# Attention seam of a two-block model: queries evacuated between rotations, two value banks taken by ACT, the mask between the kinds of score matmul

## The chip, the cores and the metric

The kernel runs on one core of one Trainium2 chip. The time is device microseconds of one execution, the median of three runs. Engines are named as in the profile: PE is TensorE (PEld its weight loads), DVE is VectorE, ACT is ScalarE, POOL is GpSimd, SP is SyncE, which issues most of the DMAs.

## The reference

A sequence of 512 tokens of width 1024 goes through two blocks in fp32. The first has an HGRN2 mixer with a gated convolution and a convolutional FFN. The second has two layers, each of FFN, mixer, FFN; the mixer of its first layer is a causal pooling, that of its second is multi-head latent attention. The change touches only this attention:

```python
cq = rmsnorm_2(u @ w_dq, q_lora_norm)                    # 512 x 256
q = jnp.einsum('bsr,rhd->bshd', cq, w_uq)                # 16 heads, 128 plain + 64 rope
q_nope = q[..., :QK_NOPE_DIM]
q_rope = apply_rope(q[..., QK_NOPE_DIM:], cos[None, :, None], sin[None, :, None])
...
s = (jnp.einsum('bqhd,bkhd->bhqk', qn_b, k_nope)
     + jnp.einsum('bqhr,bkr->bhqk', qr_b, k_rope))
s = s.astype(jnp.float32) * scale
s = jnp.where(mask[None, None], s, -jnp.inf)             # causal
p = jax.nn.softmax(s, axis=-1).astype(v.dtype)
return jnp.einsum('bhqk,bkhd->bqhd', p, v)
```

Keys and values come from a shared latent of 128 columns (`k_nope`, `v`), and one rope key of 64 is shared by all heads.

## The kernel before, in words

Every engine runs one hand-written program of its own, in order, and meets the others at counting semaphores. An instruction that waits holds all that stands behind it on its engine.

The 16 heads are done in four quarters of four heads, `attend(q)` on each engine, the first three in a loop (q is a register there) and the last written out (q is the integer 3, and `last` is true). A quarter has 14 groups of matmuls, each filling one of eight PSUM banks and counted by `groups_done`: two groups of rope queries and four of keys, computed at the end of the quarter before, then in `attend` four of values (numbers 6 to 9, in banks 6, 7, 0, 1) and four of queries (10 to 13, in banks 2 to 5). A product of fp32 data with split operands (`three`) is three matmuls, a high and a low part of each side, so a value group is three matmuls and a query group six. DVE empties the banks and counts them in `evacuated`; PE waits for that count before it reuses a bank.

The rope queries of two pairs of heads take a path of their own. DVE evacuates them to `QRr` (`take_rope`) and multiplies by the cosines into `QRt` (`rope_cosines`). SP turns the 32-row blocks of `QRr` into `QRs` with four DMAs (`turn_queries`, L618). DVE multiplies `QRs` by the sines (L2842) and adds it to `QRt` (L2846), which is the rotation. ACT writes the high part of the rotated queries (`rope_queries_hi`, L1286 and L1287), DVE the low part (`rope_queries_lo`, L2815), and SP joins the halves of each pair with two DMAs (`join_halves`, L624 and L626), counted by `rope_moved`. `rope_q` holds cosines and sines; the sign of two blocks of sines is turned once by DVE (L2796).

Score tile i of a head is 128 queries by (i+1)*128 keys in ring bank i: a plain product in fp32 (L2027, recorded as two matmuls), two rope matmuls (high and low key, L2030), and a bf16 matmul that adds the causal mask to the last block (L2032). DVE takes the maximum of each row (L2859) and scales it (L2862), ACT takes the exponential with its sum (L1315), DVE the reciprocal (L2868) and normalises (L2873), PE transposes the probabilities (L2061), DVE and ACT copy them to SBUF, and PE multiplies by the values (L2078). PE writes scores of head h+1 into a ring bank once the exponential of head h has read it.

Between its rope copies and its first exponential, ACT also converts the weights of the next quarter in the first three quarters:

```python
rope_queries_hi(q)
if not isinstance(q, int):
    rope_hi(q * 2 + (UB["attn"] + 3), q + 1, q * 14 + (GB["attn"] + 6))
    a.wait_ge(groups_done, q * 14 + (GB["attn"] + 14))
    keys_hi(q * 2 + (UB["attn"] + 2), q + 1, 0, UNIT, 4)
```

`keys_hi` (L1266, waited for at L1306) overwrites the high parts from which this quarter's values and queries are computed. POOL subtracts them from the raw weights to get the low parts (`rope_lo` L665, `split_lo` L672).

Of the kernel before, what the change touches and what calls it, by code (L numbers as in the profile page):

```python
# [9 lines left out]
ACT = mybir.ActivationFunctionType  # L10
# [119 lines left out]
def build(nc, A, out):  # L130
    ctx = ExitStack()
    with ctx:
# [238 lines left out]
        rope_key_ready = sem("rope_key_ready")  # L371
        scores_ready = sem("scores_ready")
# [107 lines left out]
        def _(sp):  # L480
# [132 lines left out]
            def turn_queries(q, taken):  # L613

                sp.wait_ge(evacuated, taken)
                for b in range(4):
                    src, dst = slice(b * 32, b * 32 + 32), slice((b ^ 1) * 32, (b ^ 1) * 32 + 32)
                    sp.dma_start(QRs[dst, :], QRr[src, :]).then_inc(qrope_turned, 16)  # L618
# [14 lines left out]
            turn_queries(0, GB["attn"] + 6)  # L633
# [147 lines left out]
        def _(a):  # L781
# [518 lines left out]

            def attend(q):

                rope_queries_hi(q)
# [68 lines left out]
        def _(pe):  # L1372
# [612 lines left out]
            def attend(q):  # L1985
# [25 lines left out]
                for x in range(4):  # L2011
                    queries(x, 10 + x)

                def scores(h, i0=0, i1=TC):

                    if h % 2 == 0:
                        pe.wait_ge(rope_moved[h // 2], q * 32 + 32)
                    for i in range(i0, i1):
                        if i == i0:
                            pe.wait_ge(evacuated, q * 14 + (gb + 11 + h))  # L2020
                        if h == 0:
                            if i == 3:
                                pe.wait_ge(evacuated, q * 14 + (gb + 12))
                        else:
                            pe.wait_ge(exp_ready, q * 16 + (4 * (h - 1) + i + 1))
                        n = (i + 1) * P
                        nc.tensor.matmul(ring[i][:, 0:n], QN[:, h * T + i * P:h * T + (i + 1) * P],  # L2027
                                         KN[:, h * T:h * T + n], start=True, stop=False)
                        for key in rope_key:
                            nc.tensor.matmul(ring[i][:, 0:n], rope_two[h][:, i * P:(i + 1) * P], key[:, 0:n],  # L2030
                                             start=False, stop=False)
                        nc.tensor.matmul(ring[i][:, i * P:n], identb[:, :], causal[:, :],  # L2032
                                         start=False, stop=True).then_inc(scores_ready, 1)
# [16 lines left out]
                scores(0)  # L2050
                for h in range(4):
                    if h < 3:
                        scores(h + 1, 0, TC - 1 if h < 2 else TC)
                    if h == 0:
                        pe.wait_ge(evacuated, q * 14 + (gb + 14))
                    for i in range(TC):
# [42 lines left out]
        def _(v):  # L2099
# [694 lines left out]
            for b in (0, 2):  # L2794
                minus = rope_q[b * 32:b * 32 + 32, T:2 * T]
                nc.vector.tensor_scalar(minus, minus, -1.0, None, ALU.mult).then_inc(sin_signed, 1)  # L2796

# [27 lines left out]
            rope_cosines(0, 4)  # L2825

            def attend(q):
# [7 lines left out]
                def take_values(n):  # L2835
                    v.wait_ge(groups_done, q * 14 + (gb + n + 1))
                    nc.vector.tensor_copy(tile(VV, n - 6), banks[n % 8][:, :]).then_inc(evacuated, 1)

                v.wait_ge(qrope_turned, q * 64 + 64)
                v.wait_ge(sin_signed, 2)  # L2840
                for j in range(2):
                    nc.vector.tensor_tensor(tile(QRs, j), tile(QRs, j), rope_q[:, T:2 * T], ALU.mult  # L2842
                                            ).then_inc(qrope_part, 1)
                for j in range(2):
# [3 lines left out]
                for j in range(2):  # L2848
                    take_values(6 + 2 * j)
                    take_values(7 + 2 * j)  # L2850
                    rope_queries_lo(q, j)
                for j in range(4):
                    take(10 + j, tile(QN, j))
# [22 lines left out]
                maxes(0)  # L2876
                normalise(0)
# [130 lines left out]
```

## Time and profile before

| | |
|---|---|
| median of three runs | 2347.74 us (2346.78 to 2347.82) |
| profiled execution | 2345.91 us, its span 2344.0 us |
| mean granted TensorE clock | 0.996 |
| PE busy | 2308.6 us (98%) |
| PEld busy | 2016.7 us (86%) |
| DVE busy | 1665.8 us (71%) |
| ACT busy | 1020.1 us (44%) |
| POOL busy | 841.4 us (36%) |

Busy time is a share of the whole span, and the attention is only its part from about 1716 to 1899 us. The quarters start their value groups at about 1718.7, 1770.2, 1814.4 and 1858.7 us. In a timeline a row is one instruction, or several of one kind in a row (xN): its start, its duration, and in brackets the idle time before it with what ended it. The duration of an instruction covers its passage through the engine, and the next one of the same engine can start a little before it is over.

### The profile page before, as it was taken

The page shows a single profiled execution, that of the slowest core. Times are in us where ns is not written, and L with a number is a line of the kernel's source. Part 1 is how long each engine was busy: PE and PEld are TensorE (multiplying, and loading weights), DVE is VectorE, ACT ScalarE, POOL GpSimd, SP SyncE. Part 2 cuts the span into 40 slices and gives each one's busy share as a digit, 9 for nine tenths or more (in the row PEclk, how much of TensorE's full clock was granted, in tenths as well). Part 3 has the DMA queues.
Part 4 walks back from the last instruction along what each step waited for, and adds up shares of the span by engine and source line. Part 5 has one row for each costly group of instructions (what it writes and reads, how often), then busy time and mean ns, then how long its engine had stood idle before and what let it go on. Part 6 is the DMA issues. An engine that isn't in the chain of part 4 may idle for free.

```text
span 2344.0 us, 33535 instructions
## 1 busy us (share of the span) xinstructions
PE 2308.6 (98%) x13510; PEld 2016.7 (86%) x13510; DVE 1665.8 (71%) x1672; ACT 1020.1 (44%) x1294; POOL 841.4 (36%) x441
## 2 busy tenths in 40 slices
PE   9999999999999999999999999999989999999998
PEld 7888788888789999979899879899967778899997
DVE  6687687772489678668587769696777743686874
ACT  5324443432355344554354454353444443453443
POOL 1321222121046446349256228356310001474561
PEclk9999999999999999999999999999999999999999
DMA  5221232332323333323342333332332222233322
GB/s 176 72 72 55 73 111 93 100 96 95 97 73 118 99 111 95 102 73 103 113 126 73 91 117 98 102 122 93 91 77 50 62 73 90 90 101 112 113 86 86
DMA packets 221332, 221.39 MB, mean 94 GB/s; under 512 B 11154, under 2 KB 217617, under 8 KB 221201
## 3 DMA queue, kind: packets, MB, share of 16 engines
q1 hardware_dynamic: 221040, 219.46, 29.8%
q8 instruction: 96, 1.57, 0.3%
q14 instruction: 36, 0.29, 0.0%
q10 hardware_dynamic: 160, 0.07, 0.0%
HBM read 213.22 MB, written 2.10 MB: 92 GB/s over the span
## 4 chain that ended last, share of the span: by engine, by line
PE 84%; POOL 5%; DVE 5%; issue 2%; ACT 2%; DMA 2%; SPq 0%; DVEq 0%; ACTq 0%; POOLq 0%
PE bank L1385 15%; PE bank L1387 15%; PE bank L1386 15%; PE bank L1379 10%; PE bank L1381 10%; PE bank L1380 10%; POOL sums L697 2%; POOL raw L698 1%; PE bank L2078 1%; PE bank L1514 1%; POOL sums L700 1%; PE bank L2027 1%; POOL sums L702 1%; PE bank L2030 1%; PE bank L2061 1%
## 5 line engine op out<-in xcount | busy, mean ns | idle before, releaser
L1379 PE MATMUL bank<-Xhi,wlo 128*128 128x256 f32 (+1 forms) x1283 | 374.2, 292 | 4.3 <-DVE Xlo L2382 2.8
L1380 PE MATMUL bank<-Xlo,whi 128*128 128x256 f32 (+1 forms) x1283 | 373.0, 291 | 0.0
L1381 PE MATMUL bank<-Xhi,whi 128*128 128x256 f32 (+1 forms) x1283 | 372.9, 291 | 0.0
L697 POOL TENSOR_TENSOR sums<-raw 128x512 f32<-128x512 f32 x72 | 147.2, 2044 | 430.5 <-DMA raw<-in_ffn_post_wg_dram 162.5
L1060 ACT ACTIVATE whi<-raw 128x2048 fp32r<-128x2048 f32 x72 | 138.3, 1921 | 370.5 <-PE bank L1387 230.7
L1379 PE MATMUL bank<-Xhi,sxlo 128*128 128x256 f32 (+1 forms) x960 | 281.0, 293 | 0.4 <-ACT kept L1099 0.2
L1380 PE MATMUL bank<-Xlo,sxhi 128*128 128x256 f32 (+1 forms) x960 | 278.9, 291 | 0.0
L1381 PE MATMUL bank<-Xhi,sxhi 128*128 128x256 f32 (+1 forms) x960 | 278.8, 290 | 0.0
L1379 PEld LDWEIGHTS bank<-Xhi,wlo 128*128 128x128 f32 x1283 | 241.8, 188 | 11.7 <-issue 4.5
L1380 PEld LDWEIGHTS bank<-Xlo,whi 128*128 128x128 f32 x1283 | 241.7, 188 | 6.5 <-issue 0.5
L1381 PEld LDWEIGHTS bank<-Xhi,whi 128*128 128x128 f32 x1283 | 241.8, 188 | 5.8
L1385 PE MATMUL bank<-xghi,wlo 128*128 128x512 f32 x592 | 232.3, 392 | 0.8 <-DVE work L2426 0.4
L2473 DVE TENSOR_TENSOR wlo<-raw,whi 128x2048 fp32r<-128x2048 f32 x72 | 211.4, 2937 | 30.2 <-ACT whi L1060 29.6
L1387 PE MATMUL bank<-xghi,whi 128*128 128x512 f32 x592 | 230.5, 389 | 0.0
L792 ACT ACTIVATE whi<-raw 128x2048 fp32r<-128x2048 f32 x68 | 130.1, 1913 | 224.2 <-PE bank L1387 224.0
L1386 PE MATMUL bank<-xglo,whi 128*128 128x512 f32 x576 | 224.2, 389 | 0.0
L2104 DVE TENSOR_TENSOR wlo<-raw,whi 128x2048 fp32r<-128x2048 f32 x55 | 127.2, 2312 | 128.9 <-ACT whi L792 128.9
L2566 DVE SCALAR_TENSOR_TENSOR xT<-bank,xT 128x512 f32<-128x512 f32 x128 | 86.2, 687 | 168.8 <-PE bank L1387 168.8
L1379 PEld LDWEIGHTS bank<-Xhi,sxlo 128*128 128x128 f32 x960 | 180.4, 188 | 6.2 <-ACT kept L1099 1.3
L1380 PEld LDWEIGHTS bank<-Xlo,sxhi 128*128 128x128 f32 x960 | 180.4, 188 | 4.8 <-issue 0.5
L1381 PEld LDWEIGHTS bank<-Xhi,sxhi 128*128 128x128 f32 x960 | 180.4, 188 | 4.4
L2476 DVE TENSOR_TENSOR sxlo<-sums,sxhi 128x1536 fp32r<-128x1536 f32 x72 | 174.2, 2420 | 0.0
(389 smaller groups left out, 5597.4 us busy)
## 6 DMA issues: line engine op xcount, KB each, us to landing
raw<-in_ffn_w_up_dram SPq DMA_DIRECT2D x22, 1024.0 KB, 5.1
raw<-in_ffn_pre_wg_dram SPq DMA_DIRECT2D x22, 1024.0 KB, 5.3
raw<-in_ffn_pre_wu_dram SPq DMA_DIRECT2D x22, 1024.0 KB, 5.4
raw<-in_ffn_post_wg_dram SPq DMA_DIRECT2D x22, 1024.0 KB, 5.4
raw<-in_ffn_post_wu_dram SPq DMA_DIRECT2D x22, 1024.0 KB, 5.4
raw<-in_ffn_pre_wd_dram SPq DMA_DIRECT2D x24, 768.0 KB, 4.8
raw<-in_ffn_post_wd_dram SPq DMA_DIRECT2D x24, 768.0 KB, 4.8
raw<-in_w_in_dram SPq DMA_DIRECT2D x13, 1024.0 KB, 5.0
```

What stands on the lines that cost most here:

```text
L697: nc.gpsimd.tensor_tensor(s1, a21, a22, ALU.add).then_inc(adds_done[h], 1)
L792: nc.scalar.activation(whi[:, s * UNIT:(s + 1) * UNIT], raw[:, s * UNIT:(s + 1) * UNIT], ACT.Copy).then_inc(whi_ready[s], 4)
L1060: nc.scalar.activation(whi[:, h * UNIT:(h + 1) * UNIT], raw[:, h * UNIT:(h + 1) * UNIT], ACT.Copy).then_inc(whi_ready[h], 2)
L1379: nc.tensor.matmul(bank, wl, x, start=first, stop=False, skip_group_check=True)
L1380: nc.tensor.matmul(bank, w, xl, start=False, stop=False, skip_group_check=True)
L1381: return nc.tensor.matmul(bank, w, x, start=False, stop=last, skip_group_check=True)
L1385: nc.tensor.matmul(bank, wlo_, xhi, start=first, stop=False)
L1386: nc.tensor.matmul(bank, whi_, xlo, start=False, stop=False)
L1387: return nc.tensor.matmul(bank, whi_, xhi, start=False, stop=last)
L2104: nc.vector.tensor_tensor(wlo[:, c], raw[:, c], whi[:, c].bitcast(F32), ALU.subtract).then_inc(wlo_ready[s], 4)
L2473: nc.vector.tensor_tensor(wlo[:, c], raw[:, c], whi[:, c].bitcast(F32), ALU.subtract).then_inc(wlo_ready[h], 2)
L2476: nc.vector.tensor_tensor(sxlo[h][:, :], sums[h][:, :], sxhi[h][:, :].bitcast(F32), ALU.subtract).then_inc(wlo_ready[h], 2)
```

## The change

On PE, three of the four query groups stand before the scores of head 0 and the fourth (`queries(3, 13)`) behind them. Each score tile is plain product, mask, rope matmuls, and the wait for the joined rope halves has moved from ahead of the head to ahead of the first tile's rope matmuls. On DVE the values 8 and 9 are taken first (each counts 2 in `evacuated`), then rotation 0, query 0, rotation 1, low part 0, query 1, low part 1, query 2; query 3 is taken behind the maxima of head 0. Each rotation is a multiply followed at once by its add. ACT takes the values 6 and 7 at the head of `attend`, counted by the new semaphore `values_act`, for which PE waits before it transposes head 0. In quarter 0 ACT issues two of the four turning DMAs. The turning of the signs moves behind `rope_cosines`. Nothing else is edited.

```diff
-            turn_queries(0, GB["attn"] + 6)
+            turn_queries(0, GB["attn"] + 6, (0, 1))
...
+            a.wait_ge(evacuated, GB["attn"] + 6)
+            for b in (2, 3):
+                src, dst = slice(b * 32, b * 32 + 32), slice((b ^ 1) * 32, (b ^ 1) * 32 + 32)
+                nc.scalar.dma_start(QRs[dst, :], QRr[src, :]).then_inc(qrope_turned, 16)
+
             def attend(q):
 
+                for n in (6, 7):
+                    a.wait_ge(groups_done, q * 14 + (GB["attn"] + n + 1))
+                    nc.scalar.activation(tile(VV, n - 6), banks[n][:, :], ACT.Copy).then_inc(values_act, 1)
                 rope_queries_hi(q)
...
-                for x in range(4):
+                for x in range(3):
                     queries(x, 10 + x)
...
-                    if h % 2 == 0:
-                        pe.wait_ge(rope_moved[h // 2], q * 32 + 32)
...
-                        for key in rope_key:
-                            nc.tensor.matmul(ring[i][:, 0:n], rope_two[h][:, i * P:(i + 1) * P], key[:, 0:n],
-                                             start=False, stop=False)
                         nc.tensor.matmul(ring[i][:, i * P:n], identb[:, :], causal[:, :],
+                                         start=False, stop=False)
+                        if h % 2 == 0 and i == i0:
+                            pe.wait_ge(rope_moved[h // 2], q * 32 + 32)
+                        nc.tensor.matmul(ring[i][:, 0:n], rope_two[h][:, i * P:(i + 1) * P], rope_key[0][:, 0:n],
+                                         start=False, stop=False)
+                        nc.tensor.matmul(ring[i][:, 0:n], rope_two[h][:, i * P:(i + 1) * P], rope_key[1][:, 0:n],
                                          start=False, stop=True).then_inc(scores_ready, 1)
...
                 scores(0)
+                queries(3, 13)
...
                         pe.wait_ge(evacuated, q * 14 + (gb + 14))
+                        pe.wait_ge(values_act, q * 2 + 2)
...
-            for b in (0, 2):
-                minus = rope_q[b * 32:b * 32 + 32, T:2 * T]
-                nc.vector.tensor_scalar(minus, minus, -1.0, None, ALU.mult).then_inc(sin_signed, 1)
...
             rope_cosines(0, 4)
+            for b in (0, 2):
+                minus = rope_q[b * 32:b * 32 + 32, T:2 * T]
+                nc.vector.tensor_scalar(minus, minus, -1.0, None, ALU.mult).then_inc(sin_signed, 1)
...
-                v.wait_ge(qrope_turned, q * 64 + 64)
-                v.wait_ge(sin_signed, 2)
-                for j in range(2):
+                def rotate(j):
                     nc.vector.tensor_tensor(tile(QRs, j), tile(QRs, j), rope_q[:, T:2 * T], ALU.mult
                                             ).then_inc(qrope_part, 1)
-                for j in range(2):
                     v.wait_ge(qrope_part, q * 4 + (j + 3))
                     nc.vector.tensor_tensor(tile(QRt, j), tile(QRt, j), tile(QRs, j), ALU.add
                                             ).then_inc(qrope_ready, 1)
-                for j in range(2):
-                    take_values(6 + 2 * j)
-                    take_values(7 + 2 * j)
-                    rope_queries_lo(q, j)
-                for j in range(4):
-                    take(10 + j, tile(QN, j))
+
+                take_values(8)
+                take_values(9)
+                v.wait_ge(qrope_turned, q * 64 + 64)
+                v.wait_ge(sin_signed, 2)
+                rotate(0)
+                take(10, tile(QN, 0))
+                rotate(1)
+                rope_queries_lo(q, 0)
+                take(11, tile(QN, 1))
+                rope_queries_lo(q, 1)
+                take(12, tile(QN, 2))
...
                 maxes(0)
+                take(13, tile(QN, 3))
                 normalise(0)
```

## Rows read from the trace of the kernel before

**Rows 1.** PE's waits over the whole span: total us, times, longest.
```profile
PE bank L2027 <- DVE QN L2833: 9.0, 4, 6.7
```
**Rows 2.** Timeline of PE, quarter 0: start us, us, instruction, idle before.
```profile
1733.73 0.80 PE L2027 MATMUL bank<-KN,QN 128*128 128x128 f32 x2 [6.72 <-DVE QN L2833]
```
**Rows 3.** Windows: stretch, length, busy PE, PEld, DVE, ACT, POOL, clock, DMA, GB/s.
```profile
1733.70:1736.00 2.30, 2.27 (x9) 2.09 (x9) 2.12 (x5) 0.11 (x1) 2.30 (x1) 0.50 0.49 114
...
635.00:636.00 1.00, 1.00 (x6) 1.00 (x6) 1.00 (x2) 0.64 (x2) 0.00 (x0) 0.50 0.00 0
```
**Rows 4.** Timeline of PE ahead of the second of those windows.
```profile
633.47 0.36 PE L1379 MATMUL bank<-Xhi,wlo 128*128 128x256 f32 x1 [2.80 <-DVE Xlo L2382]
```
**Rows 5.** Timeline of PE, quarter 1.
```profile
1772.95 0.39 PE L1385 MATMUL bank<-cqhi,wlo 128*128 128x512 f32 x1
...
1778.16 0.39 PE L1387 MATMUL bank<-cqhi,whi 128*128 128x512 f32 x1
1779.49 0.49 PE L2027 MATMUL bank<-KN,QN 128*128 128x128 f32 x2 [0.94 <-DVE QN L2833]
...
1783.41 0.44 PE L2027 MATMUL bank<-KN,QN 128*128 128x128 f32 x2
...
1789.25 2.39 PE L2078 MATMUL bank<-PT,VV 128*128 128x512 f32 x8 [0.31 <-DVE PT L2883]
```
**Rows 6.** Timeline of DVE, quarter 1.
```profile
1771.67 1.28 DVE L2842 TENSOR_TENSOR work<-work,rope_q 128x512 f32<-128x512 f32 x2
...
1775.27 0.69 DVE L2815 TENSOR_TENSOR work<-QRt,whi 128x512 fp32r<-128x512 f32 x1
...
1777.06 1.77 DVE L2815 TENSOR_TENSOR work<-QRt,wlo 128x512 fp32r<-128x512 f32 x1
...
1785.34 0.18 DVE L2868 RECIPROCAL rowinv<-rowsum 128x4 f32<-128x4 f32 x1 [0.85 <-ACT work L1315]
```
**Rows 7.** Timeline of ACT, quarter 1.
```profile
1773.59 0.63 ACT L1286 ACTIVATE whi<-QRt 128x512 fp32r<-128x512 f32 x1 [3.87 <-DVE QRt L2846]
...
1778.73 1.91 ACT L1266 ACTIVATE whi<-raw 128x2048 fp32r<-128x2048 f32 x1 [1.88 <-PE bank L1387]
1781.65 0.37 ACT L1315 ACTIVATE work<-bank,negmax 128x128 f32<-128x128 f32 x1 [1.01 <-DVE negmax L2862]
...
1784.53 0.69 ACT L1315 ACTIVATE work<-bank,negmax 128x512 f32<-128x512 f32 x1 [0.91 <-DVE negmax L2862]
```
**Rows 8.** Timeline of SP, quarter 1 (DMA issues).
```profile
1776.52 0.60 SPq L626 DMA_DIRECT2D whi<-work  x1
```
**Rows 9.** DMA issues, quarter 1: count, KB each, median us to landing.
```profile
whi<-work SPq DMA_DIRECT2D x2, 128.0 KB, 2.2
```
**Rows 10.** Timeline of POOL, quarter 1.
```profile
1780.78 4.55 POOL L672 TENSOR_TENSOR wlo<-raw,whi 128x2048 fp32r<-128x2048 f32 x1 [2.50 <-ACT whi L1266]
```
**Rows 11.** Timeline of POOL and DVE in the first block.
```profile
136.82 2.28 POOL L741 TENSOR_TENSOR V<-fkb 128x1024 f32<-128x1024 f32 x1 [10.57 <-DVE SC L2192]
...
137.38 2.00 DVE L2208 TENSOR_SCALAR CH<-GC,cols 128x512 f32<-128x512 f32 x1
```
**Rows 12.** One line of the kernel: durations in ns, min/median/max.
```profile
L2862 DVE TENSOR_SCALAR negmax<-rowmax x64: 153/154/156, 1735.7 to 1891.5; 128x1 f32<-128x1 f32 x64
```
**Rows 13.** Timeline of DVE and SP, quarter 0.
```profile
1715.69 0.85 DVE L2796 TENSOR_SCALAR rope_q<-rope_q 32x512 f32<-32x512 f32 x2
...
1721.01 3.21 SPq L618 DMA_DIRECT2D work<-sq  x4
...
1725.94 1.29 DVE L2842 TENSOR_TENSOR work<-work,rope_q 128x512 f32<-128x512 f32 x2 [3.76 <-DMA work<-sq]
...
1741.12 0.18 DVE L2868 RECIPROCAL rowinv<-rowsum 128x4 f32<-128x4 f32 x1 [0.85 <-ACT work L1315]
```
**Rows 14.** Timeline of DVE and PE, quarter 3.
```profile
1860.12 1.29 DVE L2842 TENSOR_TENSOR work<-work,rope_q 128x512 f32<-128x512 f32 x2
...
1877.03 2.39 PE L2078 MATMUL bank<-PT,VV 128*128 128x512 f32 x8 [0.19 <-DVE PT L2883]
```

More of the change, by code:

```diff
@@ L371, in build @@
         rope_key_ready = sem("rope_key_ready")
+        values_act = sem("values_act")
         scores_ready = sem("scores_ready")
@@ L611, in quarter_weights, with turn_queries @@
                              heads(1, NOPE, NOPE + ROPE)).then_inc(raw_ready[1], 16)
-            def turn_queries(q, taken):
+            def turn_queries(q, taken, blocks=range(4)):
                 sp.wait_ge(evacuated, taken)
-                for b in range(4):
+                for b in blocks:
                     src, dst = slice(b * 32, b * 32 + 32), slice((b ^ 1) * 32, (b ^ 1) * 32 + 32)
@@ L2836, in take_values @@
                     v.wait_ge(groups_done, q * 14 + (gb + n + 1))
-                    nc.vector.tensor_copy(tile(VV, n - 6), banks[n % 8][:, :]).then_inc(evacuated, 1)
-                v.wait_ge(qrope_turned, q * 64 + 64)
-                v.wait_ge(sin_signed, 2)
-                for j in range(2):
+                    nc.vector.tensor_copy(tile(VV, n - 6), banks[n % 8][:, :]).then_inc(evacuated, 2)
+                def rotate(j):
                     nc.vector.tensor_tensor(tile(QRs, j), tile(QRs, j), rope_q[:, T:2 * T], ALU.mult
                                             ).then_inc(qrope_part, 1)
-                for j in range(2):
                     v.wait_ge(qrope_part, q * 4 + (j + 3))
```

## The prediction, made before the change was run

> **What bounds the kernel now.** The page's busy times come first: PE is busy nearly throughout, every other engine much less (the table above). Time can come only from PE's idle time or from fewer PE cycles, and the change removes no matmul. The list of PE's waits over the whole span says where the idle time is: the largest is the first score matmul (L2027) waiting for DVE's queries, 9.0 us in four waits, 6.7 of it in one [rows 1]. That is the seam of each quarter of the attention, where the last query matmul ends and the first score waits.
>
> PE's timeline shows the seam of quarter 0: 6.72 us idle before the first score at 1733.73 [rows 2]. The granted clock behind it is 0.50, the lower of the two levels (1.2 GHz), and an idle time of 2.80 us at another place is also followed by 0.50 [rows 3, 4]. In quarter 1 the seam costs 0.94 us [rows 5]. I take quarter 1 as the model. DVE is busy without a break from 1771.67 to the first score, so DVE's order sets when scores start. After that one chain matters: scores, maxima, exponentials on ACT, reciprocal (1785.34) and normalising on DVE, transposes, and the first probability-value product (L2078) at 1789.25 [rows 5, 6]. I measure each quarter by how far its reciprocal, or that product, moves; behind the product PE has no wait worth a line until the next seam.
>
> **PE's new order.** Three query groups stand before the scores of head 0 and the fourth after them. From 1772.95 to 1778.16 are 23 spacings of 0.227 us, so one group of six matmuls is 1.36 us [rows 5]: PE is through three at 1777.03, and the moved group puts 1.36 us between the scores of heads 0 and 1. Head 0's four tiles take 3.92 us (1779.49 to 1783.41) [rows 5].
>
> **The mask between the kinds.** Same matmuls, same weights, other order. No row has the new order; I take 0. Bounds: a quarter of one 0.227 us spacing, either way, on the 16 one-block tiles, where the matmuls are too short to cover a weight load: 1 us.
>
> **DVE's new order, quarter 1.** DVE is free at 1771.67 [rows 6]. It now first wants values 8 and 9, whose last matmuls start 0.91 and 0.23 us before 1772.95 and last 0.39. The copies start at about 1772.5 and 1773.2: free at 1773.8. Two operations in a row take 0.60 and 0.69 (1.28), and one that waits for its predecessor's result must let the whole 0.69 pass [rows 6], so a rotation, now a multiply and at once its add, is 1.33 us. Rotation 0 ends at 1775.15, query 0 at 1775.75, rotation 1 at 1777.08, and the low part of rotated pair 0 at 1777.77; before it ended at 1775.27 + 0.69 = 1775.96 [rows 6]. It is 1.8 us later although ACT now takes two value banks, because it has moved behind two copies that must first be waited for, a query and the other rotation. ACT has its high part ready at about 1776.6 (from 1775.28, two copies of 0.65) and doesn't hold it; ACT's two value copies end by 1772.4 and lie in the 3.87 us that it idled [rows 7]. The low part of pair 1 would start at 1778.55 before POOL's short subtraction and lose the stretch that made it 1.77 us [rows 6]; head 2 alone wants it, so nothing comes of that.
>
> **The halves arrive late.** After the low part SP issues two transfers, the second 0.56 us behind it, and a landing takes 2.2 us, 2.3 with the wake-up behind it [rows 6, 8, 9]: 1777.77 + 0.56 + 2.3 = 1780.65. PE, ready at 1777.03, does tile 0's plain product and mask (some 0.4 us) and stands until 1780.7: 3.1 us idle. The remaining 3.6 of the 3.92 us follow: head 0's scores end at S = 1784.3, before at 1783.41.
>
> **The wait that nobody moved.** In quarters 0 to 2 ACT converts the next quarter's weights (L1266, 1.91 us) ahead of its first exponential, and waits for group 14 of the quarter, the last query (L1306). It waited for PE before as well, 1.88 us, and started 0.18 us after the last query's end (1778.16 + 0.39) [rows 5, 7], with time to spare. Now that query is computed behind the scores. Behind the waiting ACT stand all exponentials of head 0, and for each of them PE's next tile of head 1, which reuses the bank. S 1784.3, + 1.52 (last query's end), + 0.18, + 1.83 for the conversion: ACT is free at 1787.85. The exponentials, 0.37 us for the smallest tile and 0.69 for the largest, with 0.09 each for reading the sum, are 2.5 us for four in a row [rows 7]; the reciprocal starts at 1790.35 instead of 1785.34: **+5.0 us**. Query 3's evacuation on DVE (0.69) hides in DVE's own wait for these.
>
> **POOL comes into step with normalising.** POOL's subtraction starts 0.14 us after the conversion and lasts 4.55 us [rows 7, 10]. Before it ended at 1785.33, as normalising began. Now it runs from 1788.0 to 1792.6, and normalising would start at 1790.6. Bounds: the scaling of the maxima, a TENSOR_SCALAR of one column, took 0.153 to 0.156 us in all 64 cases, beside POOL too [rows 12]: 0. A TENSOR_SCALAR of 512 columns from SBUF to SBUF, started at 137.38 beside a POOL operation that ended at 139.10, took 2.00 us and ended 0.28 after it [rows 11]: then normalising waits until 1792.6, **+2.0**. That row is nearer (many columns, SBUF to SBUF), so I take 2.0. The Trainium skill (SBUF — State Buffer, Who interferes with whom) has a rule for it: GpSimd and a VectorE operation in a two-port mode shut each other out for a whole instruction, and tensor_scalar is among those that can enter the mode. By that rule the 2.0 us stand, without it the sum would be 6.0 us less; the trace agrees in the 2.00 us row.
>
> **The clock.** Idle times of 6.72 and 2.80 us were followed by work at 0.50, the 0.94 us of quarter 1 was not [rows 2 to 5]. From first score to reciprocal quarter 0 took 7.39 us (1733.73 to 1741.12), quarter 1 5.85 (1779.49 to 1785.34) [rows 2, 5, 6, 13]: 1.5 us for one fall. The 3.1 us idle time makes one in quarters 1, 2 and 3, +1.5 each; bounds 0 and, as PE stands for another 2.5 us behind the moved query, 3.0.
>
> **Quarters.** *1 and 2:* 5.0 + 2.0 + 1.5 = 8.5 each. *3* has no conversion behind it. From DVE's start at 1860.12 the same steps land the halves at 1869.1 and end the scores at 1872.8. Then PE is the path: 1.36 for the query, and what quarter 1 took from there to the product (1783.41 to 1789.25, 5.84) less 0.6 of waiting in it: 1879.4, before 1877.03 [rows 5, 14]. +2.3, and +1.5 for the clock: 3.8. *0:* the two sign operations (0.85) leave the front of DVE's chain, so the rope queries are evacuated 0.9 us earlier, at 1720.1. Two of the four turning transfers go to ACT's queue, where ACT is idle; four issues took 3.21 us, two fewer save 1.3, and the turned halves are there at about 1724.0 instead of 1725.94 [rows 13]. The Trainium skill (DMA: Bandwidth & Descriptors, Issuing engines are not separate DMA queues) says that all issuers share the same DMA engines and a second one saves issue time only. By that the 1.3 us is all there is to have; no run here has two issuers. The same steps give: low part done 1727.95, halves landed 1730.8, scores (with the lower clock, as before) until 1736.0, ACT free 1739.5, reciprocal 1742.0 against 1741.12: +0.9, and +2.0 for POOL. The conversion eats what this quarter gained.
>
> **Sum.** 2.9 + 8.5 + 8.5 + 3.8 = 23.7 us. The profiled run took 2345.91 us for its span of 2344.0; the median of the runs is 2347.74, 1.8 above it. 2347.7 + 23.7 = 2371.4, taken as 2371.
>
> **Rivals.**
> *POOL and normalising do not meet:* +23.7 - 6.0 = +17.7, 2365.4. For it the one-column row, against it the 2.00 us row. 0.18.
> *The conversion is not on the path,* if ACT gets through it in time. Quarters 1 to 3 then go as the last, 3.8 each, and quarter 0, bound by PE from 1736.0 on, has its product at 1742.6, 2.4 earlier than the 1745.0 that its reciprocal implies: +9.0, 2356.7. Against it: the waiting instruction stands ahead of the exponentials. 0.07; in half of it, without the clock falls, +4.5, within 0.2%.
> *PE is never held* (the other side): quarter 0 gives back 6.7 and 1.5, and each other quarter its seam and some 0.6 behind it, 5 in all: 2334. Its place is the wait for the rope halves ahead of tile 0's last two matmuls. It decides from the point where they land when three queries are done, 1777.0 in quarter 1 and not 1780.65. Against it: their low part isn't computed until 1777.8. 0.04.
> The forecast has the rest, 0.71, with a range of its own of 2366 to 2378.
>
> **How the numbers follow.** A measurement of this kernel can tell about 0.2%, 4.7 us, from no change. Low end: no meeting with POOL (-6.0), no clock falls (-4.5), mask -1: +12.2, 2360, and 2358 to take in some of the small rivals. High end: a second fall in each quarter (+6), landings 0.6 us slower in each (+2.4), mask +1: +33, cut to 2380, since they won't all come. Slower 0.92, same 0.04 (half the second rival), faster 0.04.
>
> **What the profile after would show.** L1266 starting behind the head-0 scores in quarters 0 to 2, the first exponential right behind it; PE idle for about 3 us at tile 0's rope matmul and about 2.5 us at head 1's first tile, released by ACT; the first normalising instruction of those quarters stretched to 1 to 2 us; a clock below 1 in every quarter; quarter 0 about even. The prediction is wrong if the first exponential does not wait behind L1266, or if quarter 1's low part of pair 0 ends by 1776 and no rope wait shows.

## The result and the profile after

The changed kernel takes 2370.2 us (median of 4 runs, 2366.59 to 2378.85) against 2347.78 (4 runs, 2346.78 to 2347.98): a ratio of 1.0099, 95% interval 1.0076 to 1.0122. It is slower by 22.4 us; the forecast was 2371. The profiled execution took 2366.59 us for a span of 2364.8, 20.8 more than before's.

All of it is in the attention's four quarters. The table gives the start (us) of each quarter's first probability-value product (L2078 before, L2090 after); for quarter 3 it gives the start of the output projection behind it instead. What a quarter adds is the growth of the lag between the two kernels since the quarter ahead of it. Quarter 0's figure adds the 0.31 us by which this trace starts the values of quarter 0 earlier (1718.38 against 1718.69).

| quarter | before | after | this quarter adds | forecast |
|---|---|---|---|---|
| 0 | 1745.03 | 1750.05 | 5.3 | 2.9 |
| 1 | 1789.25 | 1801.10 | 6.8 | 8.5 |
| 2 | 1833.48 | 1852.29 | 7.0 | 8.5 |
| 3 | 1898.45 | 1919.52 | 2.3 | 3.8 |

PE's waits over the whole span of the changed kernel (total us, times, longest), in the place of the one wait of before [rows 1]:
```profile
PE bank L2040 <- DMA whi<-work: 14.0, 4, 4.3
PE bank L2034 <- ACT work L1324: 7.5, 3, 2.5
PE bank L2073 <- DVE work L2887: 2.2, 3, 1.8
...
PE bank L2034 <- DVE QN L2844: 0.8, 1, 0.8
```
The wait for DVE's queries is nearly gone (9.0 to 0.8 us). What stands in its place is larger: 14.0 us for the rotated halves, once in each quarter, and 7.5 us for ACT, once in each of quarters 0 to 2.

PE's timeline of quarter 1 after the change, to be laid beside [rows 5]; this quarter starts 5.00 us later than before's:
```profile
1782.03 0.38 PE L2034 MATMUL bank<-KN,QN 128*128 128x128 f32 x2
1782.25 0.22 PE L2036 MATMUL bank<-causal,identb 128*128 128x128 bf16 x1
1785.67 0.33 PE L2040 MATMUL bank<-whi 128*128 128x128 f32 x1 [3.20 <-DMA whi<-work]
...
1789.32 0.39 PE L1394 MATMUL bank<-cqhi,wlo 128*128 128x512 f32 x1
...
1793.34 0.49 PE L2034 MATMUL bank<-KN,QN 128*128 128x128 f32 x2 [2.49 <-ACT work L1324]
...
1797.83 1.55 PE L2073 MATMUL bank<-ident,work 128*128 128x128 f32 x10 [0.20 <-DVE work L2887]
```
PE does tile 0's plain product and its mask and then stands 3.20 us until the halves land. The moved query starts at 1789.32, which is where head 0's scores end. Head 1's first tile then waits 2.49 us for an exponential.

ACT, POOL and DVE in the same stretch, to be laid beside [rows 6, 7, 10]:
```profile
1791.03 1.91 ACT L1267 ACTIVATE whi<-raw 128x2048 fp32r<-128x2048 f32 x1 [6.90 <-PE bank L1396]
1792.85 0.35 ACT L1324 ACTIVATE work<-bank,negmax 128x128 f32<-128x128 f32 x1
...
1793.08 4.52 POOL L673 TENSOR_TENSOR wlo<-raw,whi 128x2048 fp32r<-128x2048 f32 x1 [7.55 <-ACT whi L1267]
...
1782.08 0.68 DVE L2823 TENSOR_TENSOR work<-QRt,whi 128x512 fp32r<-128x512 f32 x1
...
1795.01 0.18 DVE L2882 RECIPROCAL rowinv<-rowsum 128x4 f32<-128x4 f32 x1 [3.43 <-ACT work L1324]
1795.22 3.46 DVE L2887 TENSOR_SCALAR work<-work,rowinv 128x128 f32<-128x128 f32 x4
```
ACT stood 6.90 us in front of the conversion, where before it stood 1.88, and the first exponential runs right behind it. DVE then waits 3.43 us for the exponentials instead of 0.85. Normalising takes 3.46 us instead of 1.27. The line's own durations in that quarter (ns, min/median/max) say how:
```profile
L2887 DVE TENSOR_SCALAR work<-work,rowinv x4: 341/441/2467, 1795.2 to 1798.2; 128x128 f32<-128x128 f32 x1, 128x256 f32<-128x256 f32 x1, 128x384 f32<-128x384 f32 x1, 128x512 f32<-128x512 f32 x1
```
One of the four took 2.47 us, from 1795.22 to 1797.69, and POOL's subtraction ended at 1793.08 + 4.52 = 1797.60; the others were not held.

Windows of the changed kernel, columns as in [rows 3]. The first two are in quarter 1, head 0's scores and the later part of head 1's (behind the 2.49 us wait); the third is a stretch of quarter 0 behind the same wait, the last the whole attention:
```profile
1785.70:1789.30 3.60, 3.60 (x17) 2.46 (x18) 1.73 (x6) 0.00 (x0) 0.00 (x0) 1.00 0.21 50
1795.30:1797.80 2.50, 2.33 (x6) 1.03 (x5) 2.50 (x2) 0.00 (x0) 2.31 (x1) 0.54 0.00 0
...
1747.00:1750.00 3.00, 3.00 (x8) 1.69 (x8) 1.67 (x5) 2.33 (x8) 0.00 (x0) 0.53 0.90 255
...
1715.00:1925.00 210.00, 183.59 (x862) 132.89 (x861) 145.02 (x327) 89.50 (x212) 17.35 (x6) 0.96 0.20 54
```
Behind 3.20 us of idle time the scores of quarter 1 ran at full clock. The fall came after the second wait, and there it cost nothing: PE, though slowed, still stood 0.20 us at the transposes (L2073) for normalising, which POOL was holding up. At full clock it would only have stood there longer, 1.79 us (experiment 6). In quarter 0 the clock fell twice, and the second fall reached the transposes and the product.

### The profile page after: what moved, and what is told of

Its sections match the earlier page's. It is cut to its first block, busy times and chain, and to the rows that moved or that the text cites. A ratio compares the mean times of both kernels' runs of the same rounds, so it can differ in the third digit from the quotient of the medians.

```text
span 2364.8 us, 33547 instructions
## 1 busy us (share of the span) xinstructions
PE 2314.5 (98%) x13510; PEld 2020.5 (85%) x13510; DVE 1669.4 (71%) x1664; ACT 1022.1 (43%) x1302; POOL 842.0 (36%) x441
## 4 chain that ended last, share of the span: by engine, by line
PE 84%; POOL 5%; DVE 4%; DMA 2%; issue 2%; ACT 2%; SPq 0%; DVEq 0%; ACTq 0%; POOLq 0%
PE bank L1394 16%; PE bank L1396 16%; PE bank L1395 16%; PE bank L1388 10%; PE bank L1389 10%; PE bank L1390 10%; POOL sums L698 2%; POOL raw L699 1%; PE bank L2090 1%; PE bank L2034 1%; PE bank L1523 1%; POOL sums L701 1%; POOL sums L703 1%; PE bank L2073 1%; PE bank L2040 0%
```

## The experiments

Each was timed against the kernel before in the same session (medians of before 2347.32, 2347.6 and 2347.48). The question behind them: which edits cost, which gain, and does a version exist that keeps the gain?

**1. One edit alone.** The kernel before, with only the fourth query group moved.
```diff
-                for x in range(4):
+                for x in range(3):
                     queries(x, 10 + x)
...
                 scores(0)
+                queries(3, 13)
...
-                for j in range(4):
+                for j in range(3):
                     take(10 + j, tile(QN, j))
...
                 maxes(0)
+                take(13, tile(QN, 3))
```


> The kernel before, with one edit: query 3 is computed behind the scores of head 0 and evacuated behind their maxima. Main theory (the weight conversion L1266, which waits for that query, holds the exponentials): quarter 1 keeps its first score at the old distance, its reciprocal comes about 4.1 us later (1.52 to the last query's end, 0.18, 1.83 for the conversion, 2.5 for four exponentials, against 1.9 before), and the normalising meets POOL for 2.2 us more: +6.3 us in each of quarters 0 to 2, about +0.7 in the last: +19 to +20, 2367 (up to 3 more by the clock). Rival (the late halves are what costs, and filling PE with a query behind the scores is harmless): -1 to +2, 2346 to 2350.

Measured: 2368.32 us (2366.61 to 2372.21), ratio 1.0089 (1.0074 to 1.0105). This edit by itself costs 21.0 us, where the whole change costs 22.4. Its DVE timeline, quarter 1, shows both waits:
```profile
1795.13 0.18 DVE L2869 RECIPROCAL rowinv<-rowsum 128x4 f32<-128x4 f32 x1 [3.43 <-ACT work L1315]
1795.34 3.45 DVE L2874 TENSOR_SCALAR work<-work,rowinv 128x128 f32<-128x128 f32 x4
```
The rivals in which the conversion is not on the path fall.

**2. The same edit undone.** The changed kernel, with the query back ahead of the scores.
```diff
-                for x in range(3):
+                for x in range(4):
                     queries(x, 10 + x)
...
                 scores(0)
-                queries(3, 13)
```


> The changed kernel with query 3 computed ahead of the scores again; its evacuation stays behind the maxima. Main theory: PE does the query inside its 3.2 us wait for the halves, ACT converts before the first score, POOL is done before the normalising. What is left is the lateness of the halves: +0.9 in quarters 1 and 2, +1.5 in 3, -2 in 0: about +1, 2349 (2346 to 2351). Rival (late halves and the ACT value copies are the cost): the 3.2 us idle time per quarter stays on the path: 2360 or more.

Measured: 2351.16 us (2349.25 to 2353.73), ratio 1.0017 (1.0008 to 1.0026): 19 us come back. The reciprocal of quarter 1 waits for little:
```profile
1786.75 0.18 DVE L2881 RECIPROCAL rowinv<-rowsum 128x4 f32<-128x4 f32 x1 [0.21 <-ACT work L1324]
```
That is 2 us above what was expected. All the other edits together (with query 3 still evacuated behind the maxima) are a small loss of 3.8 us. PE's waits name it:
```profile
PE bank L2040 <- DMA whi<-work: 10.0, 4, 4.3
```

**3. The order on ACT alone.** The changed kernel, the conversion and its wait moved behind head 0's exponentials; PE's order stays as changed.
```diff
-                    a.wait_ge(groups_done, q * 14 + (GB["attn"] + 14))
-                    keys_hi(q * 2 + (UB["attn"] + 2), q + 1, 0, UNIT, 4)
...
                 exps(0)
+                if not isinstance(q, int):
+                    a.wait_ge(groups_done, q * 14 + (GB["attn"] + 14))
+                    keys_hi(q * 2 + (UB["attn"] + 2), q + 1, 0, UNIT, 4)
```


> The changed kernel with ACT's conversion of the next quarter's weights moved behind the exponentials of head 0; query 3 stays behind the scores. Main theory (the place of the conversion in ACT's queue is the cost, and not the late query): reciprocal of head 0 back to about 1.9 us behind the scores, PE bound by its own work from there, POOL now beside the normalising of head 1 for up to 1 us: +2.3 in quarter 3, +2 to +3 in 1 and 2, about 0 in 0: 2354 to 2357 against 2370. Rival (the late query is the cost wherever the conversion is): no gain, 2366 or more.

Measured: 2354.37 us (2352.21 to 2355.0), ratio 1.0028 (1.0016 to 1.0039). So 16 us come back without touching PE's order: it is not the late query that costs, but the exponentials queued behind an instruction that waits for it. Head 1's first tile no longer waits for ACT. POOL, which follows the conversion, no longer meets normalising either, which is back at 1.27; the 16 us hold both:
```profile
1787.84 1.27 DVE L2888 TENSOR_SCALAR work<-work,rowinv 128x128 f32<-128x128 f32 x4
```

**4. POOL out of step.** The changed kernel, POOL's subtraction held back until head 0 is normalised.
```diff
                 rope_lo(q * 2 + (UB["attn"] + 3))
+                pool.wait_ge(probs_ready, q * 16 + 4)
                 split_lo(q * 2 + (UB["attn"] + 2), 0)
```


> The changed kernel; POOL's subtraction waits until head 0 is normalised. Main theory (the two can't run together): the first normalising instruction of quarters 0 to 2 goes back from about 2.5 us to 0.29, -2.2 in each, -6.6: 2363 to 2365. Rival (the stretched instruction hides behind the other work or has another cause): no change, 2370.

Measured: 2367.12 us (2363.96 to 2368.41), ratio 1.0082 (1.0068 to 1.0096), 3.1 us below the changed kernel's first median and 3.9 below its second (experiment 7). The mechanism is there: in quarter 1 POOL starts at 1794.06, behind normalising, and that takes its 1.28.
```profile
1792.65 1.28 DVE L2888 TENSOR_SCALAR work<-work,rowinv 128x128 f32<-128x128 f32 x4
```
But of the 3 x 2.19 = 6.6 us only about half comes back in the medians, and the two traced spans differ by 2.7 us. The traces say where the rest went. From head 1's first tile to the first product the quarters 0 to 2 took 8.93, 7.76 and 7.76 us in the changed kernel and take 5.58, 6.71 and 5.58 here. Where no fall touches either kernel (quarter 2) that is the 2.19 us less; quarter 0 gains more, since the changed kernel had a fall there, and quarter 1 less, since PE at the lower clock now has no wait to hide in. Together it is 6.6 us less. But in quarter 2 the clock now falls behind the wait for the halves, where it did not in the changed kernel's trace. These are PE's rope matmul and the 6 us from there on, first in this kernel, then in the changed one (window columns as above):
```profile
1833.21 0.47 PE L2041 MATMUL bank<-whi 128*128 128x128 f32 x1 [3.26 <-DMA whi<-work]
1833.20:1839.20 6.00, 5.99 (x15) 3.62 (x16) 1.74 (x6) 0.00 (x0) 0.00 (x0) 0.50 0.12 29
...
1836.85 0.33 PE L2040 MATMUL bank<-whi 128*128 128x128 f32 x1 [3.26 <-DMA whi<-work]
1836.80:1842.80 6.00, 5.18 (x23) 3.43 (x23) 3.28 (x9) 0.58 (x1) 0.00 (x0) 1.00 0.14 31
```
After the same 3.26 us of idle time one ran at 0.50 and the other at 1.00. From this rope matmul to head 1's first tile it took 10.75 us here and 7.68 there, so the fall gave back 3.1 us. Whether falls also explain the medians is not shown: the two kernels' falls differ from run to run.

**5. The mask alone.** The kernel before, with the mask between the kinds and the wait at the first tile's rope matmuls.
```diff
-                    if h % 2 == 0:
-                        pe.wait_ge(rope_moved[h // 2], q * 32 + 32)
                     for i in range(i0, i1):
...
-                        for key in rope_key:
-                            nc.tensor.matmul(ring[i][:, 0:n], rope_two[h][:, i * P:(i + 1) * P], key[:, 0:n],
-                                             start=False, stop=False)
                         nc.tensor.matmul(ring[i][:, i * P:n], identb[:, :], causal[:, :],
-                                         start=False, stop=True).then_inc(scores_ready, 1)
+                                         start=False, stop=False)
+                        if h % 2 == 0 and i == i0:
+                            pe.wait_ge(rope_moved[h // 2], q * 32 + 32)
+                        nc.tensor.matmul(ring[i][:, 0:n], rope_two[h][:, i * P:(i + 1) * P], rope_key[0][:, 0:n],
+                                         start=False, stop=False)
+                        nc.tensor.matmul(ring[i][:, 0:n], rope_two[h][:, i * P:(i + 1) * P], rope_key[1][:, 0:n],
+                                         start=False, stop=True).then_inc(scores_ready, 1)
```


> The kernel before with two edits: the mask between the plain product and the rope matmuls, and the rope wait ahead of the first tile's rope matmuls. In the changed kernel's trace the new order takes 0.04 us more on a one-block tile, 0.03 more on two blocks, nothing on three and 0.02 less on four; the wait is not what ends last before the scores of quarters 0 to 2. Main theory: no difference, within 1 us. Rival (the switch between kinds costs or saves weight loads): 3 us either way over the 64 tiles.

Measured: 2347.95 us, ratio 1.0 (0.9991 to 1.0009). The mask's new place costs and gives nothing that an interval of 2 us either way would show. (11 of its 12 executions lie between 2346.41 and 2350.5 us; one took 13237 us, for which nothing here gives a cause. The median doesn't rest on it.)

**6. The clock.** The changed kernel with matmuls that nothing reads, 12 ahead of the wait for the rope halves and, in quarters 0 to 2, 10 behind the moved query, so that PE is hardly ever idle there.
```diff
+                        if h == 0 and i == i0:
+                            pe.wait_ge(values_act, q * 2 + 2)
+                            for _ in range(12):
+                                nc.tensor.matmul(banks[6][:, :], ckhi[:, 0:P], ckhi[:, :], start=True, stop=True)
                         if h % 2 == 0 and i == i0:
                             pe.wait_ge(rope_moved[h // 2], q * 32 + 32)
...
                 queries(3, 13)
+                for _ in range(0 if last else 10):
+                    nc.tensor.matmul(banks[6][:, :], ckhi[:, 0:P], ckhi[:, :], start=True, stop=True)
```


> The changed kernel with matmuls that nobody reads, into a free bank: 12 ahead of the rope wait of each quarter (2.7 of its 3.2 to 4.3 us) and 10 behind query 3 in quarters 0 to 2 (2.3 of 2.5 us). They lie in PE's waits, so without a clock effect the time stays 2368 to 2370. Main theory (the waits lower the clock, at places that differ from run to run, and that is the spread of 12 us): the granted clock stays near 1.00 through the attention, the median falls by 2 to 6 us, to 2364 to 2368, and the runs lie closer together. Rival (the waits cost only themselves): no fall, same spread.

Measured: 2365.92 us (2363.45 to 2368.09), ratio 1.008 (1.0067 to 1.0093). Windows of the attention, of this kernel:
```profile
1715.00:1925.00 210.00, 197.59 (x953) 145.57 (x952) 145.00 (x327) 89.64 (x212) 17.41 (x6) 1.00 0.21 57
```
And its transposes of quarter 1, behind the wait for normalising:
```profile
1794.85 1.55 PE L2079 MATMUL bank<-ident,work 128*128 128x128 f32 x10 [1.79 <-DVE work L2893]
```
From the first rope matmul to the first product the quarters 0 to 2 take 15.45, 15.46 and 15.46 us here, and took 19.10, 15.43 and 15.44 in the trace of the changed kernel: there the falls cost 3.65 us in quarter 0 and nothing in quarters 1 and 2, where they lay inside the wait for normalising.

**7. The changed kernel again**, unedited, to have a second median beside this one.

> The changed kernel unedited, once more, for its median and its spread beside the filled one (2365.9, 2363.5 to 2368.1). If the clock falls were worth 3 to 4 us, it is at 2369 to 2371 with a wider spread; if not, at 2366.

Measured: 2371.03 us (2369.87 to 2373.09), ratio 1.0099 (1.0084 to 1.0115). Windows of the attention, and PE's timeline in quarter 1:
```profile
1715.00:1925.00 210.00, 181.60 (x838) 130.60 (x837) 143.16 (x326) 85.92 (x209) 17.36 (x6) 0.94 0.20 51
```
```profile
1800.22 2.15 PE L2073 MATMUL bank<-ident,work 128*128 128x128 f32 x9 [0.58 <-DVE work L2887]
```
With the clock at 1.00 instead of 0.94 to 0.96, and 78 matmuls more, the filled kernel's median is 4.3 and 5.1 us below the two medians of the changed one (4.1 and 5.2 if each is taken against the kernel before of its own session). That is about what the falls cost, those of quarter 0 included. In this second trace they came in other places than in the first: the transposes of quarter 1 took 2.15 us, 1.55 in the first, the clock was 0.72 in the 6 us behind quarter 2's wait for the halves, and from the first rope matmul to the first product the quarters 0 to 2 took 19.41, 16.48 and 18.32 us.

**8. The low part first.** Experiment 2 with DVE's order changed: it first turns pair 0 and computes its low part as early as the value banks let it, and the low part of pair 1, which only head 2 wants, goes last.
```diff
-                take_values(8)
-                take_values(9)
                 v.wait_ge(qrope_turned, q * 64 + 64)
                 v.wait_ge(sin_signed, 2)
                 rotate(0)
+                take_values(8)
+                take_values(9)
+                rope_queries_lo(q, 0)
                 take(10, tile(QN, 0))
                 rotate(1)
-                rope_queries_lo(q, 0)
                 take(11, tile(QN, 1))
-                rope_queries_lo(q, 1)
                 take(12, tile(QN, 2))
+                rope_queries_lo(q, 1)
```


> Query 3 ahead of the scores, and on DVE rotation 0 first, then values 8 and 9, then low part 0, query 0, rotation 1, queries 1 and 2, low part 1. If the halves set the start of the scores, they land in quarter 1 at 1775.1 + 0.56 + 2.3 = 1778.0 on the clock of the kernel before, ahead of PE's end of four queries (1778.4), and no wait is left: -1.1 in quarters 1 and 2, -0.5 in 3, -2.5 in 0, and DVE's evacuation of query 3 off the seam: about -5, 2343. If DVE's sum of work sets it and not its order: as query3_early, 2348 to 2350.

Measured: 2343.45 us (2342.85 to 2345.48), ratio 0.9983 (0.9974 to 0.9992). This is the best version, 7.7 us below experiment 2 and below both kernels. In quarters 1 to 3 the wait for the halves is gone; the one left is that of quarter 0:
```profile
PE bank L2040 <- DMA whi<-work: 3.7, 1, 3.7
...
PE bank L2089 <- DVE PT L2897: 1.9, 5, 0.9
PE bank L2034 <- DVE QN L2843: 1.8, 1, 1.8
PE bank L2072 <- DVE work L2886: 1.7, 2, 0.9
```
Of the others none reaches 2 us: DVE's evacuation of the transposes, the seam of quarter 0, and normalising. The 3.7 us belong to this execution: the last joining transfer was issued at 1727.93 and PE went on at 1732.25, 4.3 us later. In experiments 9 to 11, where DVE also turns pair 0 first, that took 2.4 us and PE waited 1.8 us in quarter 0. Why it took longer here stays open.

**9. The query late, but harmless.** DVE's order of experiment 8, the fourth query behind the scores, the conversion moved to the end of head 1 on ACT.
```diff
-                    a.wait_ge(groups_done, q * 14 + (GB["attn"] + 14))
-                    keys_hi(q * 2 + (UB["attn"] + 2), q + 1, 0, UNIT, 4)
...
+                    if h == 1 and not isinstance(q, int):
+                        a.wait_ge(groups_done, q * 14 + (GB["attn"] + 14))
+                        keys_hi(q * 2 + (UB["attn"] + 2), q + 1, 0, UNIT, 4)
```


> The order of DVE with the halves first, query 3 behind the scores of head 0 as in the change, and ACT's conversion at the end of head 1. If the idea of the fourth query behind the scores is sound once the conversion is out of the way, it fills PE's wait for the transposed probabilities (0.3 to 0.9 us a quarter) and head 0's scores start 1.36 us earlier where the halves are there: 2341 to 2343, 1 to 2 us under the version with the query early. If POOL beside the normalising of head 3 or the later weight loads on SP come onto the path: 2344 to 2350.

Measured: 2345.41 us (2342.73 to 2349.68), ratio 0.9992 (0.9984 to 1.0001). No gain over experiment 8 (the intervals overlap), where 1 to 2 us were expected. PE is done with three queries sooner and waits for the halves again:
```profile
PE bank L2041 <- DMA whi<-work: 5.0, 4, 2.0
PE bank L2035 <- DVE QN L2845: 3.3, 1, 3.3
```
The move buys nothing as long as DVE and SP set when scores start: a query in front of the scores was free cover for their wait. Experiments 3 and 2 say the same: with the query behind the wait PE stood 14.0 us at the halves, with the query in front of it 10.0, and the median is 3.2 us lower.

**10. One DMA queue.** Experiment 8 with all four turning transfers of quarter 0 issued by SP.
```diff
-            turn_queries(0, GB["attn"] + 6, (0, 1))
+            turn_queries(0, GB["attn"] + 6)
...
-            a.wait_ge(evacuated, GB["attn"] + 6)
-            for b in (2, 3):
-                src, dst = slice(b * 32, b * 32 + 32), slice((b ^ 1) * 32, (b ^ 1) * 32 + 32)
-                nc.scalar.dma_start(QRs[dst, :], QRr[src, :]).then_inc(qrope_turned, 16)
```


> The version with the halves first (2343.5), with all four turning DMAs of quarter 0 on SP again, as before the change. Main theory: the second queue saves two issues, 1.3 us, and the turned halves are what rotation 0 of quarter 0 waits for: +1.3, 2344.8. Rival (the turning isn't on the path of quarter 0, or the transfers themselves set its end): within 0.3.

Measured: 2344.74 us (2343.14 to 2347.35), ratio 0.9991 (0.9982 to 1.0): 1.3 more, with overlapping intervals. From the sign operations to the rotation this kernel needs 1726.07 - 1721.96 = 4.11 us:
```profile
1721.96 0.86 DVE L2830 TENSOR_SCALAR rope_q<-rope_q 32x512 f32<-32x512 f32 x2
...
1726.07 0.69 DVE L2845 TENSOR_TENSOR work<-work,rope_q 128x512 f32<-128x512 f32 x1 [3.25 <-DMA work<-sq]
```
and experiment 8, from 1720.33 to 1723.88, needs 3.55. But the other eight traces with two issuers need 3.23 (the changed kernel's first) to 4.32 us, the last in experiment 2:
```profile
1721.92 0.86 DVE L2835 TENSOR_SCALAR rope_q<-rope_q 32x512 f32<-32x512 f32 x2
1726.24 0.69 DVE L2850 TENSOR_TENSOR work<-work,rope_q 128x512 f32<-128x512 f32 x1 [2.14 <-DMA work<-sq]
```
The one with a single issuer lies among them. So neither the 1.3 us between the medians nor the 0.56 us between two traces shows a gain of the second issuer; that the median came out as expected is no evidence for it.

**11. The value banks on DVE again.** Experiment 8 with all four value banks copied by DVE, each counting 1 in `evacuated` again, and without PE's wait for `values_act`.
```diff
-                for n in (6, 7):
-                    a.wait_ge(groups_done, q * 14 + (GB["attn"] + n + 1))
-                    nc.scalar.activation(tile(VV, n - 6), banks[n][:, :], ACT.Copy).then_inc(values_act, 1)
...
+                take_values(6)
+                take_values(7)
                 take_values(8)
```


> The version with the halves first (2343.5), with values 6 and 7 taken by DVE again, ahead of 8 and 9. Main theory: DVE's two copies of 0.60 us stand between rotation 0 and the low part of pair 0, the halves land 1.2 us later, at 1779.2 on the clock of before, and PE's four queries end at 1778.4: about +0.8 in quarters 1 to 3 and +1.2 in 0, 2347. Rival (ACT's two copies buy nothing): 2343 to 2344.

Measured: 2348.01 us (2345.84 to 2349.97), ratio 1.0001 (0.9992 to 1.001). ACT's two banks are worth 4.6 us with DVE's order of experiment 8 (4.4 against the kernel before of each session). With the change's own order this wasn't tried.

## Why the prediction was right, step by step

**The model held.** Quarter 1 as the model, and DVE's order as what sets the scores: in the after trace the low part of pair 0 starts 1777.08 on before's clock (1782.08 - 5.00), and 1777.08 was the forecast. The halves landed for the rope matmul at 1780.67 (forecast 1780.65), and the scores ended at 1784.32 (1784.3).

**The wait that nobody moved** was forecast at 5.0 and came to 4.67 (the reciprocal at 1790.01 on before's clock, against 1785.34). The forecast took 2.5 us for four exponentials; nothing holds them behind the conversion, and they run in 2.1 (1792.85 to 1794.97). Experiments 1 to 3 show it: moving the query costs 21 us, moving it back gives 19, moving the conversion instead gives 16. Each of these holds POOL's share and that of the clock as well.

**POOL and normalising** were forecast at 2.0 and came to 2.19 in each of quarters 0 to 2. The trace of the change alone shows it (2.47 us for one instruction, ended 0.09 behind POOL's), and experiment 4 takes it away. In the medians it is worth 3 to 4 us of 6.6, and the forecast took it to be independent of the clock, which it isn't: while POOL holds normalising, PE can run slowly at no cost. By the rule weighed in the prediction (the Trainium skill: SBUF — State Buffer, Who interferes with whom) the held instruction waits for the whole of POOL's; the trace agrees here, with 1797.69 behind 1797.60.

**The clock** is the term with the wrong place. Forecast: 1.5 us in each of quarters 1 to 3, at head 0's scores, behind the wait for the halves. In the profiled run it added nothing in quarters 1 to 3: 6.8, 7.0 and 2.3 were measured, and 7.0, 7.0 and 2.3 is the forecast without that term. In quarters 1 and 2 the clock fell only behind the second wait, inside the wait for normalising, and in quarter 3 it stayed at 1.00, where the prediction had named a lower clock in every quarter as a sign. The falls cost 3.65 us in quarter 0 instead. In two other traces a fall did come behind the wait for the halves, in quarter 2 (experiments 4 and 7). On medians the falls cost 4.3 to 5.1 us in all (experiments 6 and 7); the forecast had 4.5 for quarters 1 to 3 and, for quarter 0, the 1.5 that the kernel before pays as well, 6.0 in all. So the size was near and the place was not, and the place isn't fixed from run to run.

**Quarter 0** was forecast at 2.9 and came to 5.3. (The list of signs calls it "about even", which the forecast's own sum does not.) Its times, put on before's clock by adding 0.31: the rope matmul 1731.26 (forecast 1730.8, +0.5); from there to the end of the scores 6.16 us at the lower clock (5.2, +1.0); from there to the reciprocal 5.68 (6.0, -0.3, the exponentials again); normalising +0.2; and from normalised to the product 1.2 more, in the second fall, at 0.53, that the forecast didn't have. Before rounding these are the 2.4 that were missing. The turned halves came at 1724.33, 1.61 earlier than before. The rope queries were evacuated 1.00 earlier (from 1718.70 instead of 1719.70), mostly because the sign operations had moved, and 0.61 is left, where the forecast had 1.3 for the second issuer. Experiment 10 can't show even that: the same stretch differs by 1.1 us between traces with two issuers. The page cited there (the Trainium skill: DMA: Bandwidth & Descriptors, Issuing engines are not separate DMA queues) bounds the gain by the issue time; no trace here shows more than that, and none shows a gain clear of the spread.

**Where it was luck.** In the trace quarters 1 to 3 came 4.7 us under their forecast (16.1 of 20.8), nearly all of it the clock term, and quarter 0 came 2.4 over its own, most of it the clock as well. The total hit because these errors are opposite and because the medians lie further apart (22.4 us) than the profiled spans (20.8).

**The mask:** forecast 0, measured 0 (experiment 5).

**The rivals.** The meeting of POOL and normalising took place. The conversion was on the path. PE was held at the rope halves in all four quarters, 3.2 to 4.3 us each. This last rival named the point that decides, and experiment 8 went there: with the halves down before PE was through with its queries in quarters 1 to 3, the kernel was faster than before, by 4 us and not by the 13 of the rival, as in quarter 0 PE still waits 3.7 us for the halves and 1.8 us for DVE's queries.

**Open.** What decides behind which of two waits the clock falls, whether such falls account for POOL's missing half in the medians as they do in the traces, and whether the second issuer gains anything.

## What to carry to other kernels

When work is moved later, list every instruction that waits for it, on every engine, and what is queued behind each: here a conversion that the change didn't touch (with POOL's work behind it) made 16 us of loss out of a move that could bring each quarter's scores forward by one group, 1.36 us, at most. A wait that is removed is only worth what lies between it and the next arrival; putting first on an engine what another engine needs first (experiment 8) gained what taking work off it (the change) did not. Two causes that end at the same point can't be priced one by one: with POOL in the way the lower clock cost nothing there, and without POOL it would have. And where PE must wait anyway, work placed in front of the wait is free as long as it is shorter than the wait, and placed behind it is not.

## What the runs showed of the hardware

- The same idle time is not always followed by the same clock. 3.26 us idle in quarter 2 were followed by 1.00 in one trace and by 0.50 in another (experiment 4). In quarter 1 of the changed kernel 3.20 us were followed by 1.00, and 2.49 us soon behind them by 0.54 at 1795.3, while before the change 2.80 us were followed by 0.50 [rows 3, 4]. Four executions of the changed kernel lay 12.3 us apart in one session and 3.2 in the other; four of the one before lay 1.2 apart, 21 in a later session 4.7.
- Four exponentials with their row sums take 2.1 us when nothing holds them, for 128, 256, 384 and 512 columns.
- A TENSOR_SCALAR of a 128x128 tile in SBUF, started beside POOL's subtraction, stood until that ended (2.47 us; the shortest of its line took 0.29), while the one-column form took 0.153 to 0.156 us in 64 cases, some of them beside POOL [rows 12].
- At full clock most tiles of scores, of 128 to 512 keys, took 0.51, 0.83, 1.11 and 1.43 us with a bf16 mask between two kinds of fp32 products, and 0.47, 0.79, 1.12 and 1.39 or 1.45 with the mask last.
- The two joining transfers of 128 KB in quarter 0 were down 4.3 us after the second was issued in one trace and 2.4 us in three others with pair 0 turned first (experiment 8).
